# Two transformer blocks on one core: the first shift and scale in five steps, some of their rows summed on GpSimd, parameter columns later, and a sixteen-column product turned round

## The reference: what is computed

```
mod = c @ w_ada + b_ada                        # c [2048], w_ada [2048, 12288]
shift1, scale1, gate1, shift2, scale2, gate2 = split(mod, 6)
h = rmsnorm(x, g_pre_mix) * (1 + scale1) + shift1
proj = h @ w_in                                # w_in [2048, 9472]
q_a, k_a, v_a, q_h, f_h, i_h, g_h, gate_a, gate_h = split(proj)
... attention, gated recurrence, projections, feed-forward ...

# second block
h = rms_norm(x, norm_mix_w)
proj = h @ w_in_2
q_a, k_a, v_a, q_g, k_g, v_g, r_g, gate_lr = split(proj)      # gate_lr has 16 columns
gate_logit = gate_lr @ w_gla_gate_up + b_gla_gate             # [256, 16] @ [16, 512]
... attention, gated linear attention, feed-forward, output ...
```

## Time and profile before

| | |
|---|---|
| median of 3 runs | 2892.91 us (2892.06 to 2894.61) |
| the profiled execution | 2895.45 us |
| its span in the profile | 2893.7 us |
| busy share of the span | PE 96%, PEld 87%, DVE 62%, ACT 43%, POOL 8% |
| mean granted TensorE clock | 0.98 of full speed |
| HBM traffic | 588.75 MB, mean 203 GB/s |

### The profile page before, as it was taken

The page is one execution under the profiler, slowest core; times in us unless marked ns, Lnnn a source line. Parts: engine busy times, 40 slices in busy tenths (PEclk is TensorE's granted clock), DMA queues, the critical chain, the costliest instruction groups (busy, mean ns, idle before and its releaser), DMA issues.

```text
span 2893.7 us, 44341 instructions
## 1 busy us (share of the span) xinstructions
PE 2769.4 (96%) x17650; PEld 2510.6 (87%) x17650; DVE 1790.2 (62%) x1959; ACT 1250.0 (43%) x1509; POOL 235.6 (8%) x159
## 2 busy tenths in 40 slices
PE   4799999999899999999998999998999999999998
PEld 3798888787699998899987989877999989999876
DVE  6976778689854446644466443654666644666455
ACT  2256544344443334333344453534444434444443
POOL 1010121100000010001100000100111200112000
PEclk8899999999999999999999998999999999999999
DMA  9975646698745557655576553534555565555553
GB/s 343 360 255 196 218 136 233 220 329 304 275 161 180 183 189 259 243 181 186 177 248 218 183 167 110 169 131 146 179 174 182 181 203 189 174 186 177 188 189 116
DMA packets 297940, 588.75 MB, mean 203 GB/s; under 512 B 12234, under 2 KB 17342, under 8 KB 296926
## 3 DMA queue, kind: packets, MB, share of 16 engines
q1 hardware_dynamic: 293496, 578.03, 57.9%
q10 hardware_dynamic: 4326, 9.09, 0.9%
HBM read 584.98 MB, written 2.10 MB: 203 GB/s over the span
## 4 chain that ended last, share of the span: by engine, by line
PE 89%; DVE 7%; issue 1%; ACT 1%; DMA 1%; POOL 0%; ACTq 0%; DVEq 0%; POOLq 0%
PE psum L777 14%; PE psum L779 14%; PE psum L781 14%; PE psum L766 14%; PE psum L770 13%; PE psum L768 13%; DVE ada_acc L849 3%; DVE mod_acc L636 1%; DVE w_lo L724 1%; PE bank L909 1%; PE bank L2369 1%; DMA gla_gain<-in_gla_norm_w_dram 1%; ACT w_hi L712 1%; PE bank L1215 0%; PE bank L1220 0%
## 5 line engine op out<-in xcount | busy, mean ns | idle before, releaser
L724 DVE TENSOR_TENSOR w_lo<-raw,w_hi 128x1024 fp32r<-128x1024 f32 x916 | 1194.0, 1319 | 946.9 <-ACT w_hi L712 937.4
L712 ACT ACTIVATE w_hi<-raw 128x1024 fp32r<-128x1024 f32 x916 | 951.9, 1047 | 1384.0 <-PE psum L781 628.6
L777 PE MATMUL psum<-h_hi,w_hi 128*128 128x256 f32 x3392 | 962.1, 284 | 0.2
L781 PE MATMUL psum<-h_hi,w_lo 128*128 128x256 f32 x3392 | 959.8, 283 | 0.0
L779 PE MATMUL psum<-h_lo,w_hi 128*128 128x256 f32 x3392 | 959.8, 283 | 0.0
L777 PEld LDWEIGHTS psum<-h_hi,w_hi 128*128 128x128 f32 x3392 | 651.0, 192 | 1.7 <-issue 1.4
L779 PEld LDWEIGHTS psum<-h_lo,w_hi 128*128 128x128 f32 x3392 | 651.1, 192 | 0.1
L781 PEld LDWEIGHTS psum<-h_hi,w_lo 128*128 128x128 f32 x3392 | 651.0, 192 | 0.0
L766 PE MATMUL psum<-w_hi,h_hi 128*128 128x512 f32 (+1 forms) x928 | 366.1, 395 | 8.2 <-DVE x L2047 3.8
L768 PE MATMUL psum<-w_lo,h_hi 128*128 128x512 f32 (+1 forms) x928 | 361.5, 390 | 0.0
L770 PE MATMUL psum<-w_hi,h_lo 128*128 128x512 f32 (+1 forms) x928 | 361.5, 390 | 0.0
(11 more groups left out here) (317 smaller groups left out, 2020.7 us busy)
## 6 DMA issues: line engine op xcount, KB each, us to landing
raw<-in_w_in_dram SPq DMA_DIRECT2D x120, 1024.0 KB, 5.1
raw<-in_w_ffn_in_dram SPq DMA_DIRECT2D x88, 1024.0 KB, 4.9
raw<-in_w_ffn_up_dram SPq DMA_DIRECT2D x88, 1024.0 KB, 4.9
raw<-in_w_ada_dram SPq DMA_DIRECT2D x64, 1024.0 KB, 5.1
raw<-in_w_ffn_out_dram SPq DMA_DIRECT2D x44, 1024.0 KB, 5.2
raw<-in_w_ffn_down_dram SPq DMA_DIRECT2D x44, 1024.0 KB, 5.1
ada_raw<-in_w_ada_dram SPq DMA_DIRECT2D x64, 512.0 KB, 7.6
raw<-in_w_out_dram SPq DMA_DIRECT2D x32, 1024.0 KB, 5.1
```

What stands on the lines that cost most here:

```text
L712: nc.scalar.activation(w_hi[:, slot, :, 0:ncol], raw[:, rs, 2 * h:2 * h + 2, 0:ncol], ACT.Copy).then_inc(split_hi, inc)
L724: nc.vector.tensor_tensor(w_lo[:, slot, :, 0:ncol], raw[:, rs, 2 * h:2 * h + 2, 0:ncol], w_hi[:, slot, :, 0:ncol].bitcast(F32), ALU.subtra ...
L777: pe.matmul(o, fh, hi[:, k, :], start=first and f % 2 == 0, stop=False, skip_group_check=True)
L781: mm = pe.matmul(o, fl, hi[:, k, :], start=False, stop=last, skip_group_check=True)
```

## The change

- Quarters become five steps, `STEPS`: three of four blocks of h, then two of two blocks each. A unit of the two short steps is still 1 MB, now 4 blocks of 128 rows by 256 columns of each vector, so DVE takes four instructions of [128, 512] for it, and there are four units a step. The matching units of w_in have two blocks of rows.
- `ADA_POOL`: unit 1 of step 0, units 0 and 4 of steps 1 and 2, and unit 0 of steps 3 and 4 are summed by GpSimd, in an accumulator of its own (`ada_acc_pool`), by a multiply in place and an add. PE sums both accumulators. Each kind of unit has its own semaphore, and SP's load of a unit waits for the owner of the unit four before it.
- The turning of the convolution's rows and the bias comes after x's transposes on PE and after unit 6 of step 0 on DVE.
- GpSimd's masks come after its units.
- The sixteen-column group is in the transposed form: 48 matmuls with 16 weight columns stationary and 256 tokens moving; the result is `gate_lr` itself, and `lr_tok` and its transpose go.

```diff
+STEPS = [(0, 4), (4, 4), (8, 4), (12, 2), (14, 2)]
+ADA_POOL = [(1,), (0, 4), (0, 4), (0,), (0,)]
...
         def ada_sum_pe(pe, q):
-            pe.wait_ge(sem("ada_used"), 4 + 8 * (q + 1))
+            nk = STEPS[q][1]
             pe.wait_ge(bank_free[0], fill("ada", 0, q))
-            for n in range(8):
-                mm = pe.matmul(bank[:, 0, n:n + 1], ada_acc[:, q % 2, n // 4, (n % 4) * P:(n % 4 + 1) * P],
-                               ones[:, 0:1], start=(n == 0), stop=(n == 7), skip_group_check=True)
+            for acc, by_pool in ((ada_acc_pool, True), (ada_acc, False)):
+                last = max(u for u in range(ada_units(q)[0]) if (u in ADA_POOL[q]) == by_pool)
+                pe.wait_ge(sem(ada_owner(q, last)[0]), ada_owner(q, last)[1])
+                for c in range(2 * nk):
+                    mm = pe.matmul(bank[:, 0, c:c + 1], acc[:, q % 2, c // nk, (c % nk) * P:(c % nk + 1) * P],
+                                   ones[:, 0:1], start=by_pool and c == 0,
+                                   stop=not by_pool and c == 2 * nk - 1, skip_group_check=True)
...
+        def ada_pool(pool, chain, q, u):
+            nk = STEPS[q][1]
+            done, count = ada_owner(q, u)
+            first = u == ADA_POOL[q][0]
+            acc = ada_acc_pool[:, q % 2, :, 0:nk * P]
+            pool.wait_ge(ada_full[u % 4], 32 * ((ada_units(q)[1] + u) // 4 + 1))
+            if first and q >= 2:
+                pool.wait_ge(bank_full[0], filled("ada", 0, q - 2))
+            for kk in range(8 // nk):
+                k = 8 // nk * u + kk
+                tile = ada_tiles(q, u)[:, kk]
+                into = acc if first and kk == 0 else tile
+                chain(nc.gpsimd.tensor_scalar(into, tile, cols[:, ROW["c"] + k:ROW["c"] + k + 1], None, ALU.mult))
+                if not (first and kk == 0):
+                    chain(nc.gpsimd.tensor_tensor(acc, acc, tile, ALU.add))
+            pool.sem_inc(sem(done), 1)
...
             def load_ada(q, u):
-                sp.wait_ge(sem("ada_used"), 8 * q + u + 1)
+                k0, nk = STEPS[q]
+                rows_ = 8 // nk
+                before = ada_before(q, u)
+                if before:
+                    sp.wait_ge(sem(ada_owner(*before)[0]), ada_owner(*before)[1])
...
             for u in range(8):
                 load_ada(0, u)
-            for q in range(1, 4):
+            for q in (1, 2):
                 for u in range(8):
                     load_ada(q, u)
                     if u % 2:
                         load_first(q - 1, u // 2)
+            for u in range(4):
+                load_ada(3, u)
+                load_first(2, u)
+            for u, ready in enumerate(((0,), (1, 2), (3,), ())):
+                load_ada(4, u)
+                for g in ready:
+                    load_first(3, g)
             for g in range(4):
-                load_first(3, g)
+                load_first(4, g)
...
             ph = plan.first
             for u in range(8):
                 if u == 2:
                     normed_dve(dve, 0)
                 ada_dve(dve, 0, u)
-            for q in range(1, 4):
+                if u == 6:
+                    late_columns_dve()
+            for q in (1, 2):
                 for u in range(8):
                     ada_dve(dve, q, u)
                     if u == 1:
                         first_h_dve(dve, chain, q - 1)
                     if u % 2:
                         split_w_lo(dve, ph, 0, *first_unit(q - 1, u // 2))
-            first_h_dve(dve, chain, 3)
+            for u in range(4):
+                ada_dve(dve, 3, u)
+                if u == 0:
+                    first_h_dve(dve, chain, 2)
+                split_w_lo(dve, ph, 0, *first_unit(2, u))
+            for u, ready in enumerate(((), (0,), (1, 2, 3), ())):
+                ada_dve(dve, 4, u)
+                if u == 0:
+                    first_h_dve(dve, chain, 3)
+                for g in ready:
+                    split_w_lo(dve, ph, 0, *first_unit(3, g))
+            first_h_dve(dve, chain, 4)
             for g in range(4):
-                split_w_lo(dve, ph, 0, *first_unit(3, g))
+                split_w_lo(dve, ph, 0, *first_unit(4, g))
...
             rms_pool(pool, chain, 0)
+            pool.wait_ge(bank_free[0], emptied("cols", 0))
+            for q in range(len(STEPS)):
+                for u in ADA_POOL[q]:
+                    ada_pool(pool, chain, q, u)
...
-            for q in range(4):
+            for q in range(len(STEPS)):
                 pe.wait_ge(sem("first_lo"), q + 1)
                 for g in range(4):
                     if q < 3 and g == 3:
                         ada_sum_pe(pe, q + 1)
                     first_products(pe, q, g)
+                if q == 3:
+                    ada_sum_pe(pe, 4)
...
-                        products(pe, ph, 0, g, h_hi, h_lo, transposed=g < 4 or g in (6, 7), part=part)
+                        products(pe, ph, 0, g, h_hi, h_lo, transposed=g < 4 or g in (6, 7, 8), part=part)
...
-                            nc.scalar.activation(lr_tok[:], ps[:, :, 0:RANK], ACT.Copy).then_inc(free, 1)
+                            nc.scalar.activation(gate_lr[:], ps[0:RANK, 0, 0:TOK], ACT.Copy).then_inc(free, 1)
```

More of the change, by code:

```diff
@@ L68, with ada_units, ada_owner, ada_before @@
 FFN_PARTS = [(0, 6), (6, 5)]
+STEPS = [(0, 4), (4, 4), (8, 4), (12, 2), (14, 2)]
+ADA_POOL = [(1,), (0, 4), (0, 4), (0,), (0,)]
+def ada_units(q):
+    n = [KD * nk // 8 for _, nk in STEPS]
+    return n[q], sum(n[:q])
+def ada_owner(q, u):
+    name = "ada_pool" if u in ADA_POOL[q] else "ada_used"
+    same = [(q_, u_) for q_ in range(q + 1) for u_ in range(ada_units(q_)[0])
+            if (q_, u_) <= (q, u) and (u_ in ADA_POOL[q_]) == (u in ADA_POOL[q])]
+    return name, len(same)
+def ada_before(q, u):
+    every = [(q_, u_) for q_ in range(len(STEPS)) for u_ in range(ada_units(q_)[0])]
+    n = every.index((q, u)) - 4
+    return every[n] if n >= 0 else None
 class Phase:
-    def __init__(self, plan, iters, groups, mod=None, quarters=False):
+    def __init__(self, plan, iters, groups, mod=None, steps=None):
         self.iters, self.groups = iters, groups
@@ L103, in weight_unit @@
                 self.halves.append((g, j, h // 2, k0 + h))
-        if quarters:
-            for k0 in range(0, KD, KU):
-                for g, (kt, cols) in enumerate(groups):
-                    weight_unit(g, k0, kt, cols)
-            self.end = [len(self.halves) - 2 * (len(groups) - 1 - g) for g in range(len(groups))]
+        if steps:
+            for k0, nk in steps:
+                for g, (_, cols) in enumerate(groups):
+                    weight_unit(g, k0, k0 + nk, cols)
+            self.end = [len(self.halves) - steps[-1][1] // 2 * (len(groups) - 1 - g)
+                        for g in range(len(groups))]
             groups = []
@@ L150, in __init__ @@
             self.use.append(self.qper[g % 2])
-            if group is not None and not (quarters and g > 1):
+            if group is not None and not (steps and g > 1):
                 self.qper[g % 2] += 1
@@ L215, in __init__ @@
         half = (ATT_W // P, COLS)
-        self.first = Phase(self, 1, [full, full, (KD, 2 * KV_W), full], quarters=True)
+        self.first = Phase(self, 1, [full, full, (KD, 2 * KV_W), full], steps=STEPS)
         self.mix_in = Phase(self, 1, [None] * 4 + [full] * 7
@@ L493, in build_program @@
         gate_lr = place("gate_lr", 62, [RANK, TOK])
-        lr_tok = place("lr_tok", 63.5, [P, TT, RANK])
         vg = place("vg", 24, [P, TT, A2])
@@ L791, in first_products @@
             ph = plan.first
-            for h in range(2):
-                idx = 2 * (len(ph.groups) * q + g) + h
+            for idx in range(*first_unit(q, g)):
                 _, slot, inc, m, _, _, _, ncol = ph.half(0, idx)
@@ L838, in ada_dve @@
+        def ada_dve(dve, q, u):
+            if u in ADA_POOL[q]:
+                return
+            nk = STEPS[q][1]
+            done, count = ada_owner(q, u)
+            first = all(n in ADA_POOL[q] for n in range(u))
+            acc = ada_acc[:, q % 2, :, 0:nk * P]
+            dve.wait_ge(ada_full[u % 4], 32 * ((ada_units(q)[1] + u) // 4 + 1))
+            if first and q >= 2:
                 dve.wait_ge(bank_full[0], filled("ada", 0, q - 2))
-            for kk in range(2):
-                k = 2 * u + kk
+            for kk in range(8 // nk):
+                k = 8 // nk * u + kk
@@ L853, in first_h_dve @@
+                if kk < 8 // nk - 1:
+                    ins.then_inc(sem("ada_order"), 1)
+                    ADA_ORDER[0] += 1
+                else:
+                    ins.then_inc(sem(done), 1)
+        ADA_ORDER = [0]
         def first_h_dve(dve, chain, q):
+            k0, nk = STEPS[q]
+            part = slice(k0, k0 + nk)
             dve.wait_ge(bank_full[0], filled("ada", 0, q))
             nc.vector.tensor_tensor(
```

(17 more changed lines are left out.)

106 lines of the change are left out of this document (44 added, 62 removed).

## The result

The changed kernel takes 2902.89 us (median of 8 runs, 2901.43 to 2904.01), the kernel before, run beside it, 2894.48 (8 runs, 2892.06 to 2896.99). The ratio is 1.0029, 95% interval 1.0018 to 1.0039: **slower by 0.3%, 8.4 us**. The forecast was 2895.3, no change that can be told. The time lies in the range given (2870 to 2906), but that range is wide, and the time is nearer to rival B (2905) than to the forecast.

What follows compares the result with a forecast made beforehand. DVE was taken to bound the first stage, with transfers close behind, and PE all that follows. +11.7 us for the first stage and -9.3 for the sixteen-column group made +2.4, so 2895.3 us in the median, range 2870 to 2906.

Steps and rivals of the forecast that it cites:

- rival B: First stage: GpSimd's multiply costs DVE as much as its add (1.9 us), +9, and SP's queue adds; 2905, chance 0.18.
- Step 1: Start of first stage: parameter columns moved behind unit 6 bring the first h from 47.0 to 43.5 us, -3.5.
- The sentence on SP's queue: First stage: loads queued behind GpSimd's units are late by little while DVE is late; 0 us, bounds 0 and 4.
- Steps 2 to 5: First stage, DVE: relief by GpSimd -13 us, slowing by GpSimd +27, extra h and half splits +6.8, more instructions +3.
- steps 4 and 5: First stage, DVE: h and four half splits ahead of the last step, +6.8; four instructions a unit, not two, +3.
- Step 6: End of first stage: PE's sum over the last step is no longer hidden under a split, +2.5 us.
- The tail: First stage after the last bias add: h 2.5 us, first split 1.2, PE's products 9.9, lower clock 1.5.
- Part two: Sixteen-column group on PE: 48 matmuls of 256 tokens instead of 96, and no transpose of lr_tok; -9.3 us.
- A: First stage: GpSimd doesn't slow DVE and the transfers bind; -10 us there, 2874 in all, chance 0.27.
- C: First stage: GpSimd slows only DVE's splits, not ada_acc's instructions; 12 us less slowing, 2885, chance 0.10.
- the bound of -6.5: Sixteen-column group: the least gain, with the lower clock throughout, 48 matmuls at 0.21 us plus 2.3.
- Its sign for a wrong sum: First stage: the forecast's sum is wrong if the first h begins far from 43.5 us.

Runs made afterwards that it cites:

- the memsets: Changed kernel with three memsets in place of each multiply and add of GpSimd's units, their part of scale and shift left out: 2893.42 us, ratio 0.9994.
- the decoys: Changed kernel with all sums on VectorE, five steps, and GpSimd doing its multiplies and adds on scratch tiles beside it: 2917.41 us, ratio 1.0072.
- the multiplies alone: Changed kernel with all sums on VectorE, five steps, and GpSimd doing only its multiplies, no adds, on scratch tiles: 2896.25 us, ratio 1.0006.

## Why the prediction was off, step by step

- **Step 1, the earlier start: failed.** The late columns do what they were to do (43.3 without GpSimd's units, forecast 43.5). But the prediction let the first unit on GpSimd ride along as one "which DVE would only have waited for". It lasted 9.65 us and held SP's queue for 11.7, and the first bias add came at 48.27: +4.8. The sentence on SP's queue set this at 0 with an upper bound of 4. It reasoned that late loads are covered as long as VectorE is itself late, which holds in the middle of the stage (no wait of VectorE's for ada_raw from 50 to 164 us in the changed kernel) and not at its start, where VectorE is ahead of the transfers. The kernel with that one unit (48.07) shows it, and the memsets (47.86) show that holding the loads is enough for it; exclusion by itself would delay the first bias add as well where VectorE is relieved of nothing (50.76 in the kernel with the decoys).
- **Steps 2 to 5: right to 1 us, which is also as fine as one trace can tell.** The last sum was forecast at 160.3 (162.8 less 2.5) from 43.5 on, 116.8 us; it was in at 164.1 from 48.27 on, 115.8. From first to fourth bias add the changed kernel needs 11.0 us more than the one without GpSimd (98.0 against 87.0). The prediction's terms for its four units there, -10.4 of relief and +21.5 of exclusion, give 11.1. Without GpSimd, the time from first bias add to last sum is 102.7 us (43.28 to 145.96), where steps 4 and 5 alone give 102.8. The price of exclusion held, and the decoys show that it is exclusion: the same operations on tiles nobody uses. Some luck is in the closeness: the 0.9 for a multiply was borrowed from another operation (a cast) and measures 0.6 to 0.9, the 2.15 for an add measures 1.7 to 2.4.
- **Step 6, TensorE's sum: mis-sized.** 2.5 taken, 5.34 measured: +2.9. It was said to stand behind step 3's last group, but its price was taken from the sum alone.
- **The tail:** from last bias add to the next phase 16.7 us, forecast 15.1: +1.6. The trace has a gap of 4.25 and more products at the lower clock there; a difference of this size is also within what two traces of one stage show.
- **The sum:** 11.7 + 4.8 - 1.0 + 2.9 + 1.6 = 20.0, measured 19.8.
- **Part two: right.** -9.3 forecast, -10.1 in the trace, -7.9 by the medians of the kernel with it alone. The gap was forecast at 3.1 us and measured 3.11. The 1.2 us for a lower clock behind it were not needed in the changed kernel (granted 1.00 from 1790 to 1810); but in two of the thirteen executions with the turned group, the five steps without GpSimd and the multiplies alone, the granted clock was 0.82 in the ten us from kg's copy on and below 0.7 in the next five, and kg's copy to tokbuf's took 41.3 us instead of 39.3.
- **The rivals.** A and C fall: sums are lengthened as well as splits (6.05 for 5.3). B gave the sign and nearly the time, with one of its two mechanisms: the queue costs 4.8, above the bound of 4, but the multiply does not cost as much as the add, so that its time is near by luck in part.
- **Two slips in the sums** change nothing: by rival B's own prices its ten multiplies come to +10 and not +9, and the bound of -6.5 in part two leaves out the 0.5 for the transpose (-7.0).

Of the signs that the prediction named, four came as said: from 40 to 180 us full-width sums took 1.44 us in the mean and full-width splits 1.53, the transfers ran at 338 GB/s, VectorE never idled for them from 60 to 130 us, and the sixteen-column group had its gap. Its sign for a wrong sum came too: the first h began at 48.3, far from 43.5.

On the rule that was weighed: where GpSimd reads, VectorE's sums with two tile inputs are lengthened (6.78 and 9.24 for 5.30), and where it only writes they are not (5.30 beside memsets). The Trainium skill, "SBUF — State Buffer", section "SBUF: two separate sides", says just this, and the traces agree. The prediction gives the section's rule with "for their whole duration"; in the traces that holds for the one add that can be seen alone, and not for a multiply. At 48.46 in the changed kernel a small instruction of VectorE's with two tile inputs takes 2.19 us instead of 0.16 and ends at 50.65, together with GpSimd's add of 48.30 (2.34 us). A multiply beside which VectorE idled took 2.85 us, and two of them, 6.4 us long, cost four sums 1.5 us. The same section has a VectorE operation in a mode that uses two ports blocked by any GpSimd operation; four one-input operations at 3.53 us instead of 1.38 beside memsets agree with that, if those are such operations, which no run here shows.

Open: how exclusion and held loads share the 16.0 us in the changed kernel itself, since the kernels that take them apart change VectorE's load too. An estimate: the decoys' 29.4, less seven units' relief of 2.6 each, leave 11.2 of the 16.0, and the other 4.8 are what the first bias add is late by. Open too is whether fewer, later units on GpSimd with more buffers for w_ada could come out even, which was not tried.

## What to carry to other kernels

Work moved to GpSimd is paid for twice: in VectorE's own time, operation by operation (here some 5.4 us a unit for each 2.6 us saved: four units made the stretch 11.0 us longer though they took 10.4 off it), and in the order of a queue, when a load must wait for the slower engine's buffer and all later loads wait behind it. Ask where the relieved engine is ahead of its transfers: there the second price is due in full. And when a step is halved to start the next engine sooner, place the small operation that releases the second half (here eight matmuls) ahead of the long group, or the half step gives back what it won: without GpSimd this move was worth 6 us, and turned five steps from 3 us slower than four quarters into 3 us faster.

## What the hardware showed beyond this

- A multiply of 128x1024 by a column of scalars took GpSimd 2.84 to 4.85 us in the changed kernel, no less than an add (2.34 to 3.16), and yet it costs VectorE less than half as much (0.74 against 1.97 us where two of each were timed beside the same four sums). The time that an operation of GpSimd's lasts does not give its price to VectorE: the add of 2.34 us held a VectorE instruction until its own end, while a VectorE sum at 47.07, beside the multiply of 45.38 to 48.22, took its usual 1.28 us.
- The multiplies' and adds' prices add up: 11.2 and 20.0 us at the fourth bias add apart, 31.6 together.
- Memsets of GpSimd's, which read nothing, leave VectorE's two-input operations as they are and slow some of its one-input ones: 3.53 us for four of 128x256 instead of 1.38, but 0.75, the usual time, for one of 128x1024 at 80.03 beside the same memsets.
